# Mixture-of-experts stage of a hybrid decoder trunk: light experts turn their gated values one group later in a bank of their own, heavy experts keep weight tiles stationary, and heavy windows come in two sizes

## What is computed

```python
D_MODEL, SEQ, DEPTH = 1024, 512, 2
D_FF, N_EXPERTS, TOP_K, D_FF_EXPERT = 3072, 8, 2, 3584

def swiglu(x, w1, w3, w2):                      # layer 0
    h = silu(x @ w1) * (x @ w3)
    return h @ w2

def moe_swiglu(x, w_router, w1, w3, w2):        # layer 1
    top_vals, top_idx = lax.top_k(x @ w_router, TOP_K)
    gates = softmax(top_vals)
    ...                                         # each token goes to its two experts
    h = silu(xblk @ w1[e]) * (xblk @ w3[e])
    ...                                         # (h @ w2[e]) * gate, added per token
    return out

h = x
for layer in range(DEPTH):
    h = h + hybrid_mixer(rms_norm(h, g), ...)   # gated convolution and RG-LRU groups
    hn = rms_norm(h, g)
    h = h + (swiglu(hn, ...) if layer % 2 == 0 else moe_swiglu(hn, ...))
return rms_norm(h, final_g)
```

## Time and profile before

| | |
|---|---|
| median of 3 runs | 2249.91 us |
| the profiled execution's own time | 2247.89 us, span 2246.2 us |
| TensorE matmul, busy | 2072.2 us (92%), 9575 instructions |
| TensorE weight load, busy | 1711.8 us (76%) |
| VectorE, ScalarE, GpSimd, busy | 1534.1, 1198.1, 81.9 us |
| mean DMA rate | 218 GB/s |
| chain that ended last | TensorE 87%, VectorE 5%, DMA 2% |

### The profile page before, as it was taken

The page is one execution under the profiler, slowest core; times in us unless marked ns, Lnnn a source line. Parts: engine busy times, 40 slices in busy tenths (PEclk is TensorE's granted clock), DMA queues, the critical chain, the costliest instruction groups (busy, mean ns, idle before and its releaser), DMA issues.

```text
span 2246.2 us, 30134 instructions
## 1 busy us (share of the span) xinstructions
PE 2072.2 (92%) x9575; PEld 1711.8 (76%) x9576; DVE 1534.1 (68%) x1662; ACT 1198.1 (53%) x1492; POOL 81.9 (4%) x121
## 2 busy tenths in 40 slices
PE   5989999999979884999999999999999998999991
PEld 4767788888867673788788878787888787878881
DVE  6885666666658852566666688787665897876655
ACT  4442555555544430555455577676554776765543
POOL 1001000000000002000000000000000000000002
PEclk9999999999989996999999999999999999999996
DMA  7221866566532222566666599999666999996643
GB/s 231 85 66 56 277 188 192 181 188 194 182 119 80 70 88 73 188 224 224 240 223 225 198 354 375 340 372 328 224 224 206 353 373 335 372 341 226 222 159 127
DMA packets 245652, 489.72 MB, mean 218 GB/s; under 512 B 16564, under 2 KB 86308, under 8 KB 245604
## 3 DMA queue, kind: packets, MB, share of 16 engines
q1 hardware_dynamic: 236288, 461.43, 59.9%
q0 software_dynamic: 7936, 27.03, 3.6%
q10 hardware_dynamic: 1380, 0.61, 0.1%
HBM read 473.80 MB, written 15.22 MB: 218 GB/s over the span
## 4 chain that ended last, share of the span: by engine, by line
PE 87%; DVE 5%; issue 4%; DMA 2%; ACT 1%; POOL 1%; ACTq 0%; DVEq 0%; POOLq 0%
PE PS L1152 84%; PE PS L1387 1%; DMA raw<-in_expert_w 1%; DVE wlo L594 1%; DVE PS L666 1%; PE PS L1169 1%; PE PS L1390 1%; ACT whi L324 1%; DVE OV L627 1%; DMA OV<-in_norm_mix_g 0%; DVE XN L611 0%; POOL SM L1006 0%; POOL l_rows L1092 0%; DVE OV L790 0%; DMA raw<-y_rows,addr 0%
## 5 line engine op out<-in xcount | busy, mean ns | idle before, releaser
L1152 PE MATMUL PS<-whi,XN 128*128 128x512 f32 x3616 | 1123.4, 393 | 9.8 <-DVE XN L803 4.9
L594 DVE TENSOR_TENSOR wlo<-raw,whi 128x1024 fp32r<-128x1024 f32 x882 | 1034.6, 1219 | 138.9 <-ACT whi L324 133.5
L324 ACT ACTIVATE whi<-raw 128x1024 fp32r<-128x1024 f32 x882 | 886.3, 1052 | 108.2 <-DMA raw<-in_expert_w 54.8
L1152 PEld LDWEIGHTS PS<-whi,XN 128*128 128x128 f32 x3616 | 681.6, 189 | 155.9 <-issue 15.5
L1152 PE MATMUL PS<-wlo,XN 128*128 128x512 f32 x2144 | 772.4, 391 | 0.0
L1152 PE MATMUL PS<-XN,whi 128*128 128x512 f32 x1408 | 478.5, 400 | 5.2 <-DVE XN L611 4.7
L1152 PEld LDWEIGHTS PS<-wlo,XN 128*128 128x128 f32 x2144 | 404.2, 189 | 82.5
L1152 PE MATMUL PS<-XN,wlo 128*128 128x256 f32 (+1 forms) x1088 | 341.2, 314 | 0.0
L1152 PEld LDWEIGHTS PS<-XN,whi 128*128 128x128 f32 x1408 | 266.0, 189 | 72.1 <-issue 6.4
L1152 PEld LDWEIGHTS PS<-XN,wlo 128*128 128x128 f32 x1088 | 206.1, 189 | 14.9
L488 ACT ACTIVATE XN<-PS 128x512 fp32r<-128x512 f32 x56 | 33.5, 598 | 192.0 <-PE PS L1390 151.7
(11 more groups left out here) (187 smaller groups left out, 1034.7 us busy)
## 6 DMA issues: line engine op xcount, KB each, us to landing
raw<-in_expert_w SPq DMA_DIRECT2D x672, 512.0 KB, 5.2
raw<-in_ffn_w SPq DMA_DIRECT2D x144, 512.0 KB, 3.7
raw<-in_w_in SPq DMA_DIRECT2D x40, 512.0 KB, 4.8
raw<-in_w_out SPq DMA_DIRECT2D x16, 512.0 KB, 4.3
y_rows<-OV POOLq DMA_DIRECT2D x8, 512.0 KB, 5.1
y_rows<-OV POOLq DMA_DIRECT2D x1, 3072.0 KB, 11.6
RES<-in_x SPq DMA_DIRECT2D x4, 512.0 KB, 5.6
x_tok<-OV POOLq DMA_DIRECT2D x4, 512.0 KB, 2.9
```

The lines of the kernel that those rows point to most:

```text
L324: act.activation(whi[:, u0 % CONV, half(h)], raw[:, r, half(h)], ACT.Copy).then_inc(s["hi_done"], 1)
L594: dve.tensor_tensor(wlo[:, w, half(h)], raw[:, u0 % RAW, half(h)], whi[:, w, half(h)].bitcast(F32), ALU.subtract).then_inc(s["lo_done"], 1)
L1152: return pe.matmul(out_, lhsT, rhs, start=start, stop=stop, skip_group_check=True)
```

## The change

For a **light** visit, `m_T` of a group moves from the end of the group to between the two `m_up` of the next one, and its result goes to PSUM bank 1, which nothing else in a light visit uses. `hid_ok` is then waited for ahead of `m_down`, no longer ahead of w3's `m_up`. ScalarE's and VectorE's lists follow.

For a **heavy** visit, `heavy_up` keeps 128 x 128 weight tiles stationary and streams the window's `n` tokens, high and low part side by side: `2n` columns behind `whi`, `n` behind `wlo`, four hidden tiles in PSUM banks 0 to 3. Both up-projections use these same four banks. The result has hidden features in rows, and `m_T` is gone. ScalarE copies the low columns out (`low_columns`), VectorE adds (`heavy_sum`), gates, and the splits `heavy_hi` and `heavy_lo` follow from SBUF. The down-projection stays as it is, with `2m` instead of 128 columns of the second block, m = n - 128.

`SIZES` has 128, 160 and 192: visits 1, 4 and 7 (140, 151, 144 tokens) take n = 160, visit 0 (175 tokens) takes 192. `gT`, `gT_ext` now both stand ahead of the last `m_down` of a visit.

```diff
+SIZES = (P, 160, WIN)
...
+        XX = XF[:, 0:2 * KD * WIN].rearrange("p (a k n) -> p a k n", a=2, k=KD)
...
-            def m_group(i, g, ext, first):
+            def light_group(i, g, first):
 
                 pe.wait_ge(s["a_free"], i * GROUPS + g + 1)
-                m_up(i, g, -2, 0, ext)
-                pe.wait_ge(s["hid_ok"], i * GROUPS + g + 1)
-                m_up(i, g, 0, 1, ext)
+                m_up(i, g, -2, 0)
+                m_T(i, g - 1)
+                m_up(i, g, 0, 1)
                 if first:
                     pe.wait_ge(s["y_evac"], i * 2 + 4)
-                m_down(i, g, 2, first, False, ext)
-                m_T(i, g, ext)
+                pe.wait_ge(s["hid_ok"], i * GROUPS + g + 1)
+                m_down(i, g, 2, first, False, 0)
...
+            def heavy_up(i, g, n0, part, n, free):
+
+                for q in range(2):
+                    u = MOE_BASE + n0 + q
+                    w = u % CONV
+                    for t in range(4):
+                        if q == 0 and t % 2 == 0 and free:
+                            pe.wait_ge(s[("w3_sum", "w1_sum")[part]],
+                                       i * (2 * GROUPS) + g * 2 + (2 * part - 1 + t // 2))
+                        for kk in range(4):
+                            if t == 0 and kk % 2 == 0:
+                                pe.wait_ge(s["lo_done"], i * (2 * UNITS) + g * 12 + (2 * u + kk // 2 + 1))
+                            k, a = 4 * q + kk, slice(kk * GROUP + t * P, kk * GROUP + (t + 1) * P)
+                            mm(PS[:, t, 0:2 * n], whi[:, w, a], XX[:, :, k, 0:n], k == 0, False)
+                            ins = mm(PS[:, t, 0:n], wlo[:, w, a], XX[:, 0, k, 0:n], False, k == KD - 1)
+                        if q and t == 1:
+                            ins.then_inc(s["up_half"], 1)
+                    ins.then_inc(s["unit_used"], 1)
...
+            def heavy_group(i, g, n, first):
+
+                heavy_up(i, g, -2, 0, n, True)
+                heavy_up(i, g, 0, 1, n, True)
+                if first:
+                    pe.wait_ge(s["y_evac"], i * 2 + 4)
+                pe.wait_ge(s["hid_ok"], i * GROUPS + g + 1)
+                m_down(i, g, 2, first, False, n - P)
...
+            def low_columns(i, g, u, part, n):
+
+                low = heavy_tiles(n)[0]
+                for p in range(2):
+                    if p == 0:
+                        act.wait_ge(s["up_half"], i * (2 * GROUPS) + g * 2 + (part + 1))
+                    else:
+                        act.wait_ge(s["unit_used"], i * UNITS + g * 6 + (CONV + u))
+                    act.activation(low[:, pair(p), :], PS[:, pair(p), n:2 * n],
+                                   ACT.Copy).then_inc(s[("w1_low", "w3_low")[part]], 1)
...
+            def heavy_sum(i, g, part, n):
+
+                low, up1, h = heavy_tiles(n)
+                for p in range(2):
+                    t = i * (2 * GROUPS) + g * 2 + (p + 1)
+                    dve.wait_ge(s[("w1_low", "w3_low")[part]], t)
+                    dve.tensor_tensor((up1, h)[part][:, pair(p), :], PS[:, pair(p), 0:n], low[:, pair(p), :],
+                                      ALU.add).then_inc(s[("w1_sum", "w3_sum")[part]], 1)
...
+            def heavy(i, n):
+
+                m = n - P
+                m_split(i, 0, 5, 6)
+                heavy_sum(i, 0, 0, n)
+                m_split(i, 0, 7, 8)
+                heavy_sum(i, 0, 1, n)
+                heavy_lo(i, 0, n)
+                with dve.Fori(1, GROUPS - 1) as g:
+                    m_split(i, g, 3, 4)
+                    heavy_sum(i, g, 0, n)
+                    m_split(i, g, 5, 6)
+                    heavy_sum(i, g, 1, n)
+                    m_split(i, g, 7, 8)
+                    heavy_lo(i, g, n)
```

More of the change, by code:

```diff
@@ new lines, in next_x, with light @@
+            def next_x(i):
+                x_split(i + 1)
+                x_split_ext(i + 1)
+                m_split(i, GROUPS - 1, 8)
+            def light(i):
+                silu(i, 0, 2)
+                m_split(i, 0, 5, 6, 7, 8)
+                with act.Fori(1, GROUPS - 1) as g:
+                    m_split(i, g, 3, 4)
+                    silu(i, g, 0)
+                    hidden_hi(i, g - 1)
+                    m_split(i, g, 5, 6, 7, 8)
+                g = GROUPS - 1
+                m_split(i, g, 3, 4)
+                silu(i, g, 0)
+                hidden_hi(i, g - 1)
+                m_split(i, g, 5, 6, 7)
+                hidden_hi(i, g)
+                next_x(i)
+                for n in ("w1_low", "w1_silu", "w3_low"):
+                    act.sem_inc(s[n], 2 * GROUPS)
+                act.sem_inc(s["y_part"], 1)
@@ L528, in visit @@
+            def visit(i, n):
+                if n == P:
+                    light(i)
+                else:
+                    heavy(i, n)
+                act.wait_ge(s["unit_used"], i * UNITS + (CONV + UNITS))
+                act.wait_ge(s["y_stored"], i * 32 + 16)
                 act.activation(yt[:, 0, :].rearrange("p (a n) -> p a n", a=2), PS[:, 4:6, :],
                                ACT.Copy).then_inc(s["y_evac"], 1)
[L530 to L531 removed]
+                m_split(i, GROUPS - 1, 9, 10)
@@ L934, in _ @@
             wn, ad = r3[11], r3[13]
-            step(dve.tensor_scalar(cum, count, float(P), None, ALU.is_gt))
+            step(dve.tensor_scalar(cum, count, float(SIZES[0]), None, ALU.is_gt))
+            step(dve.scalar_tensor_tensor(cum, count, float(SIZES[1]), cum, ALU.is_gt, ALU.add))
             dve.tensor_copy(sizes[:, :], cum[0:1, :]).then_inc(s["sizes_ok"], 1)
@@ new lines, in heavy @@
+            def heavy(i, n):
+                pe.wait_ge(s["glo_done"], i * 3 + 3)
+                heavy_up(i, 0, 0, 0, n, False)
+                heavy_up(i, 0, 2, 1, n, True)
+                heavy_group(i, 1, n, True)
+                with pe.Fori(2, GROUPS) as g:
+                    heavy_group(i, g, n, False)
+                pe.wait_ge(s["w3_sum"], i * (2 * GROUPS) + 2 * GROUPS)
+                gT(i + 1)
+                gT_ext()
+                pe.wait_ge(s["hid_ok"], i * GROUPS + (GROUPS + 1))
+                m_down(i, 0, UNITS - 2, False, True, n - P)
+                pe.sem_inc(s["T_ready"], GROUPS)
```

277 lines of the change are left out of this document (134 added, 143 removed).

## The result

The changed kernel takes 2281.64 us, the median of four runs (2277.82 to 2287.25), beside 2249.93 for the kernel before: a ratio of 1.0145, with a 95% interval of 1.0132 to 1.0157. Forecast were 2189 us and a range of 2150 to 2245. The prediction was wrong, in sign too.

A forecast was written before the change was run, and what follows sets the result against it. TensorE, busy 92% of the span, was taken as the bound. Savings of 36.3 (visits 1, 4, 7), 5.8 (visit 0) and 18.6 us (light visits), together 60.7, turned 2247.9 into 2187.2; 2.0 for the median gave 2189 us, range 2150 to 2245.

The forecast's parts named there:

- Pairs of matmuls: Heavy up-projections: a wide and a narrow matmul together take 0.263 us at n = 160, 0.291 at n = 192.
- Both rivals with dear pairs: Heavy visits, slower: narrow weight load not hidden (8%, 2314 us), or narrow fp32r matmul takes several passes (8%, 2494 us).
- its two terms: Heavy pair at n = 160: 0.148 us for 320 columns, 0.115 us for the narrow matmul, taken near a weight-load floor.
- the stage's start: Visit 0: 2.4 us beyond groups, transposes and waits, kept in its forecast of 198.5 us against 204.3.
- The drain inside a visit: Heavy groups: emptying w1's banks for w3's first pair makes TensorE wait 0.1 us per group.
- The forecast tie: Heavy groups: w1's drain takes 4.2 us, and TensorE's second half of w1 also 4.2 us.
- The rival with a late drain everywhere: Every heavy group waits because ScalarE's and VectorE's lists slip 1.5 us: 27 to 35 us, total 2224; chance 10%.
- The start of a heavy visit: TensorE waits 4.2 us for w1's sum behind unit splits, 4.9 in visit 1; 4.5 taken, none in visit 0.
- The clock behind it: After the wait at a heavy visit's start, a lowered granted clock adds 1.7 us.
- Light visits: Moving `m_T` leaves a 1 us wait at `m_down`: 120.9 us each, 483.6 against 502.2, 18.6 us saved.
- light visits give nothing back: Light visits hardly have spare DMA rate, so their 18 us saving is lost: total 2207 us; chance 12%.

The follow-up runs named there:

- the kernel with two sizes: The changed kernel with only 128 and 192 columns, so two bodies in each engine's loop: 2242.69 us, ratio 0.997 to the kernel before.
- the other reordering: Two-size kernel with w1's drain ahead of unit 6's split in a heavy visit's first group: 2228.76 us; together with unit 4's split moved: 2217.11 us.
- the longer three-width code: Changed kernel with three widths on TensorE alone, ScalarE and VectorE with one heavy body of 192 columns: 2225.4 us; with both reorderings of splits 2213.66 us.

## Why the prediction was wrong

**Pairs of matmuls: right.** The start of w1 in visit 4 (start, duration) steps by 0.26 us, against 0.263:

```profile
1555.06 0.35 PE L1243 MATMUL PS<-XN,whi 128*128 128x320 f32 x1
1555.25 0.23 PE L1243 MATMUL PS<-XN,wlo 128*128 128x160 f32 x1
1555.32 0.35 PE L1243 MATMUL PS<-XN,whi 128*128 128x320 f32 x1
```

With 192 columns, in the kernel with two sizes, the step is 0.285, against 0.291:

```profile
890.44 0.36 PE L1239 MATMUL PS<-XN,whi 128*128 128x384 f32 x1
890.64 0.25 PE L1239 MATMUL PS<-XN,wlo 128*128 128x192 f32 x1
890.72 0.36 PE L1239 MATMUL PS<-XN,whi 128*128 128x384 f32 x1
```

Both rivals with dear pairs are out. The pair came out right, its two terms did not: start to start the wide matmul takes 0.19 us and the narrow one 0.07, where 0.148 and 0.115 were put in. The narrow one costs its columns and no more, the wide one some 0.05 more than its own, so part of the sum is luck. Visit 0, from its first matmul at 891.82, takes 197.2 us; 198.5 was forecast, with 2.4 for the stage's start in it.

**The drain inside a visit: right.** The forecast tie shows as one wait of 0.32 us (at 1598.22, and its like in the two other visits) and none in the other groups; 0.1 us a group was even too much. The rival with a late drain everywhere is out.

**The start of a heavy visit: right where the code is not late, but 15.3 and 16.6 us in the changed kernel's visits 4 and 7.** In the kernel with two sizes it is 3.15, 4.17 and 4.71 us, beside the forecast 4.2 to 4.9, though w1 lasts 0.8 us longer there with its wider pairs. The clock behind it was sized too low: those visits have 0.98 over 200 us, by estimate some 4 us instead of 1.7.

**Light visits: the size of the new wait was wrong.** The prediction named the mechanism, "the turned values' copies are queued behind the splits of units 3 and 4", and priced it at 1 us. It is 4.2 us a visit with two sizes (16.8 us in four), no less than the 14.6 us that it replaced, and the four visits came to 509 us, not 483.6. The rival "light visits give nothing back" (12%) is what happened to this part, but its reason is not: the DMA share was put forward, and moving the split of unit 4, two halves on each engine, brought (with the other reordering) the visits to within a few us of the forecast 120.9 at a still higher DMA share.

**The step that failed.** The sum prices instructions, waits and clock, and has no term for the code of a third body on each engine. The range was said to leave out "the two dear-pair rivals and little else"; this was left out. In the changed kernel three visits of n = 160 have 7 x (64 x 0.26 + 9.1) + 2.5 = 182.7 us of work each (the 2.5 for the transposes and the short waits at the end), 548; they take 604.3. Of the 56 between, 41.9 are waits at their starts (6.04, 4.02, 15.29 and 16.56 us). The light visits have 479.6 us of work and take 535.1; of these 55 us, 24.2 are the waits named `wlo` at or soon after their starts and 14.3 those at `m_down`. What remains of both, some 31 us, is mostly matmuls at the lower of the two clock levels behind the waits: after the 15.29 us of visit 4 the granted clock is 0.51 for 6.2 us, and a pair takes 0.48 us (1578.62 to 1579.10) in place of 0.26. Here the rival of the changed order of work keeps a share: the 14.3 us at `m_down` and 3 to 5 us at each heavy start stand with two bodies as well. Against the forecast the light visits are 51 us late and the heavy ones 33; visit 0's start and the stretch behind the stage make up most of the rest of the 93.

The Trainium skill has a rule that bears on this, and the prediction should have made it a rival ("Runtime: NRT & Kernel Launch", section "Instruction fetch mechanics"): "A taken branch whose target isn't in the current 2-page window forces a DMA fetch of the target page before execution can continue". The runs agree in kind: 7.2 us for one jump over a body, on TensorE. The page gives no size for such a stall. Nor does its sentence alone say when one comes: the kernel before jumps over a light or a heavy body at every visit too, and TensorE has no idle time without a releaser there.

**What stays open.** No view ties a packet of q8 or q14 to the idle stretch that it ends; that the stalls are late code rests on packets and idle time rising and falling together, engine by engine. The match is loose on q8: with two sizes it has 42 packets against 31, and TensorE's idle time without a releaser is 1.6 to 2.8 us. Counted in the programs, with weight loads apart, TensorE's loop over the experts has some 1400 instructions before and 1640 with two sizes, where hardly a stall shows, and 2250 and 2740 where they do; ScalarE's has 210 and 230 against 320 and 360, VectorE's 250 and 265 against 380 and 410. But length alone does not rank the stalls: TensorE's copy in the kernel before costs 36.0 us, while the longer three-width code shows 25.5 and 26.2 in the two kernels that have it on TensorE alone. And whether the length of the loop or the reach of single jumps in it decides was not separated. Where the stalls stand does not settle it: with never-run copies TensorE's come behind heavy visits and ScalarE's long ones behind light visits.

## What to carry to other kernels

Ahead of a specialised body inside a loop that is run on several engines, count the code as a cost: here one more body on each cost 84 us in eight iterations even when it was never entered, over twice the 34 us that narrower matmuls save here; a copy outside the loop cost 8. Where a wait is taken away by moving an operation, count what now stands ahead of it on each engine, in halves of splits, since here the wait came back whole at the next consumer. And read a wait's named releaser against that engine's own timeline: an engine that worked on time is not the cause.

## What the runs showed of the hardware

- A body of some 850 TensorE instructions (weight loads counted apart), 100 of ScalarE and 130 of VectorE, placed in the loop and never run, raised the instruction packets from 31 to 56 (q8) and from 17 to 89 (q14). By the page's MB a packet is some 16 KB on q8 and 8 KB on q14.
- A stall at a jump is 5 to 11 us on TensorE (14.6 once with its own third body alone, 16.9 once with all three), up to 15 us on ScalarE and up to 13.5 on VectorE.
- fp32r matmuls with weights stationary keep narrowing in time down to 160 columns: pairs of 320 and 160 columns step by 0.26 us and pairs of 384 and 192 by 0.285. By columns alone, at 0.227 us for 512, they would take 0.213 and 0.255, so of two weight loads, whose rows are 0.19 us long each, at most 0.05 us lies open.
